# Hybrid encoder layer on one core: attention started behind V's projection, the convolution's taps set between its rows, 256 keys for every block of queries

## What is computed

```python
xn = rmsnorm(x, g_mix)
proj = xn @ w_in + b_in                       # 1024 -> 512 a, 512 g, 512 q, 512 k, 512 v
u = a * sigmoid(g)                            # conv half
u = depthwise_conv(u, conv_w, 31 taps) + conv_b
conv_out = silu(layernorm(u) * ln_g + ln_b)
# attention half: 8 heads of 64; a query at column c sees all 8 rows and the 16 columns
# around c (clipped at the edges); bias from rpb by row and column distance
s = q @ k * 64**-0.5 + bias ; p = softmax(s) ; na_out = p @ v
h = x + concat(conv_out, na_out) @ w_out + b_out
h = h + moe(rmsnorm(h, g_ffn))                # 32 experts, 4 per token, clamped SwiGLU, 1024 wide
out = rmsnorm(h, g_final)
```

## Time and profile before

| | before |
|---|---|
| median of 3 runs | 1552.27 us (1552.17 to 1552.35) |
| the profiled execution | 1550.96 us, span 1549.1 us |
| PE / DVE / ACT / POOL busy | 1419.8 / 1316.0 / 960.7 / 332.5 us |
| last product of the projection ends | about 138 us |
| first scores read by DVE | 189.75 us |
| last product of the out-projection | about 322 us |
| last token's experts chosen | about 346 us |
| first expert's first weights on PE | 375.7 us |

### The profile page before, as it was taken

How to read it: one execution, slowest core, us unless ns; L and a number is a source line. 1 busy time by engine, 2 the same in 40 slices (tenths; PEclk the granted TensorE clock), 3 DMA queues, 4 the chain that set the end, 5 groups by cost and what they waited for, 6 DMA issues and landing times.

```text
span 1549.1 us, 19123 instructions
## 1 busy us (share of the span) xinstructions
PE 1419.8 (92%) x6476; PEld 1163.5 (75%) x6476; DVE 1316.0 (85%) x975; ACT 960.7 (62%) x707; POOL 332.5 (21%) x248
## 2 busy tenths in 40 slices
PE   5995179975899999999999999999999999999995
PEld 4884047764788888888888888888888888888874
DVE  7799543347899999999999999999999989999997
ACT  3230062232677777777777777777777777777762
POOL 5296760011111111111111111111111111111062
PEclk9998559965999999999999999999999999999998
DMA  9801320055899999999999999999999999999983
GB/s 301 311 1 28 106 97 1 1 206 202 317 377 389 389 374 383 391 382 386 395 382 385 384 391 377 381 389 385 390 378 396 382 387 379 393 374 390 389 323 96
DMA packets 85042, 479.81 MB, mean 310 GB/s; under 512 B 10731, under 2 KB 11030, under 8 KB 35862
## 3 DMA queue, kind: packets, MB, share of 16 engines
q1 hardware_dynamic: 71902, 433.14, 72.1%
q0 software_dynamic: 6944, 25.18, 4.7%
q10 hardware_dynamic: 6168, 21.13, 3.5%
HBM read 450.08 MB, written 29.33 MB: 309 GB/s over the span
## 4 chain that ended last, share of the span: by engine, by line
PE 82%; POOL 6%; DVE 4%; issue 3%; DMA 2%; ACT 2%; SPq 1%; POOLq 0%; ACTq 0%; DVEq 0%
PE pair L1691 22%; PE pair L1689 22%; PE pair L1690 22%; POOL area_t L582 3%; PE pair L1509 2%; PE pair L1510 2%; PE pair L1511 2%; PE pair L1702 2%; PE pair L1676 2%; PE pair L1669 2%; PE pair L1551 1%; DVE w_low L1184 1%; POOL ring L582 1%; PE pair L1570 1%; SPq L462 1%
## 5 line engine op out<-in xcount | busy, mean ns | idle before, releaser
L1184 DVE TENSOR_TENSOR w_low<-w_raw,w_high 128x2048 fp32r<-128x2048 f32 x380 | 864.0, 2291 | 91.7 <-ACT w_high L833 87.7
L833 ACT CAST w_high<-w_raw 128x2048 fp32r<-128x2048 f32 x380 | 728.1, 1917 | 283.4 <-PE pair L1691 283.4
L1689 PE MATMUL pair<-w_high,xT_high 128*128 128x512 f32 x1040 | 409.4, 394 | 0.0
L1691 PE MATMUL pair<-w_high,xT_low 128*128 128x512 f32 x1040 | 406.8, 391 | 0.0
L1690 PE MATMUL pair<-w_low,xT_high 128*128 128x512 f32 x1040 | 405.9, 390 | 0.0
L1691 PEld LDWEIGHTS pair<-w_high,xT_low 128*128 128x128 f32 x1040 | 196.1, 189 | 41.6
L1690 PEld LDWEIGHTS pair<-w_low,xT_high 128*128 128x128 f32 x1040 | 196.4, 189 | 40.3
L1689 PEld LDWEIGHTS pair<-w_high,xT_high 128*128 128x128 f32 x1040 | 196.3, 189 | 39.9
L1689 PE MATMUL pair<-w_high,hT_high 128*128 128x512 f32 x496 | 196.3, 396 | 0.0
L1690 PE MATMUL pair<-w_low,hT_high 128*128 128x512 f32 x496 | 193.6, 390 | 0.0
L1691 PE MATMUL pair<-w_high,hT_low 128*128 128x512 f32 x496 | 193.6, 390 | 0.0
(11 more groups left out here) (292 smaller groups left out, 1471.8 us busy)
## 6 DMA issues: line engine op xcount, KB each, us to landing
w_raw<-in_w_gate SPq DMA_DIRECT2D x128, 1024.0 KB, 7.2
w_raw<-in_w_up SPq DMA_DIRECT2D x128, 1024.0 KB, 6.5
w_raw<-in_w_down SPq DMA_DIRECT2D x128, 1024.0 KB, 7.2
y_rows<-area_m ACTq DMA_DIRECT2D x30, 512.0 KB
ring<-in_w_in SPq DMA_DIRECT2D x5, 2048.0 KB, 19.0
y_rows<-area_t SPq DMA_DIRECT2D x1, 8704.0 KB
ring<-in_w_out SPq DMA_DIRECT2D x2, 2048.0 KB, 10.5
h<-in_x SPq DMA_DIRECT2D x4, 512.0 KB, 8.8
```

Source lines behind the costliest of these rows:

```text
L833: s.copy(w_high[:, i % HIGH_RING, :], w_raw[i][:, :]).then_inc(high_ready, 1)
L1184: v.tensor_tensor(w_low[i][:, :], w_raw[i][:, :], w_high[:, i % HIGH_RING, :].bitcast(F32), ALU.subtract).then_inc(low_ready, 1)
L1689: t.matmul(to[half], tok_high, hi, start=(opens and kk == 0), stop=False)
L1691: last = t.matmul(to[half], tok_low, hi, start=False, stop=(k == KD - 1))
```

## The change

- POOL keeps only the norms' small operations up to the experts. All low parts of w_in and w_out, the tables and the scaling of LayerNorm go to DVE; SiLU is one ACT function (no Sigmoid and no multiplications on POOL); b_out is no longer added to h but enters each out-projection as one more matmul (`bout_rows`, L1601), split by one ACT and one DVE instruction.
- Every block now has 256 keys. For a middle block these are its own 128, the half block to its right and the half block to its left (`spans`, `v_mix`). A table then has 192 + 64 entries for the middle blocks.
- The taps are written out singly (`taps`) and spread: 67 between the low parts and tables of the projection's groups, 21 behind them, and two behind each of the first 18 rows of scores.
- The attention's loop on PE starts behind V; V's last block comes behind the first two pairs of scores. Scores of two heads are issued together (`qk_pair`), into four banks. All copies of transposed rows are ACT's.
- LayerNorm's steps stand inside the attention's loop (mean at step 16, variance at 21, SiLU at 28, low part at 31).
- The whole out-projection comes behind the attention's loop: first the attention half of all four blocks (each in its own two banks), then the convolution half, with `turn_xn2` (transposes for the router) between.
- SP loads expert piece 0 ahead of the out-projection's end, and pieces 1 to 4 behind it (before: 0 to 2, then 3 and 4).

The core of the diff:

```diff
-            for g_i in range(8, 20):
-                loaded, high, low = split_parts(g_i)
-                pool.wait_ge(win_high_ready, g_i + 1)
-                g.tensor_tensor(low, loaded, high.bitcast(F32), ALU.subtract).then_inc(win_low_pool, 1)
...
+            def tables(hd):
...
+                dve.wait_ge(raw_loaded, 16 * N_ROWS * (hd // 2 + 1))
+                raw = raw_bias[:, hd % 2, :].rearrange("p (r w) -> p w r", r=N_ROWS)
+                for dst, first, o, w in ((T_mid[:, hd, 0:192], QB, 0, 192), (T_mid[:, hd, 192:256], QB // 2, 192, 64),
+                                         (T_edge[:, hd, 0, :], QB, 256, 256), (T_edge[:, hd, 1, :], 0, 512, 256)):
+                    v.tensor_tensor(dst.rearrange("p (w r) -> p w r", r=N_ROWS), raw[:, first:first + w // N_ROWS, :],
+                                    mask[:, o:o + w].rearrange("p (w r) -> p w r", r=N_ROWS),
+                                    ALU.add).then_inc(tables_ready, 1)
...
+            glu(3)
+            for g in range(9, 16):
+                win_low_part(g)
+                taps(2)
+                if g % 2:
+                    tables(g - 9)
+                    tables(g - 8)
+                taps(2)
+            for g in range(16, 20):
+                win_low_part(g)
+                taps(2)
+            taps(CONV_K * CC - 2 * TAP_STEPS - taps_made[0])
...
+            for i in range(NS + 6):          # DVE
+                n = normalised_at(i, 10)
+                if n is not None:
+                    normalise(n)
                 if i < NS:
                     scores(i)
+                if i < TAP_STEPS:
+                    taps(2)
...
+                if i == CENTRE_AT:
+                    dve.wait_ge(mean_done, 1)
...
+                if i in RECIP_AT:
+                    dve.wait_ge(std_ready, 1)
...
+            for n in range(NQ - 1):          # PE
+                project_v(n)
+            pe.wait_ge(act_evac, 12)
+            qk_pair(0)
+            qk_pair(2)
+            project_v(NQ - 1)
+            pe.wait_ge(act_evac, 16)
             for i in range(NS + 5):
+                if i < NS:
+                    transpose_p(i)
+                if i % 2 == 0 and i + 4 < NS:
+                    qk_pair(i + 4)
+                if 1 <= i <= NS:
+                    pv(i - 1)
+                n = normalised_at(i, 10)
+                if n is not None:
+                    transpose_o(n)
+                if i == MEAN_AT:
+                    pe.wait_ge(conv_tap, CONV_K * CC)
+                    pe.wait_ge(attn_low_ready, 4)
...
+                if i == VAR_AT:
+                    pe.wait_ge(squared, CC)
+                    pe.wait_ge(attn_low_ready, 8)
...
+                if i == NS + 1:
+                    pe.wait_ge(s_ready, NS)
+                    project_attn(0)
+                if i == NS + 2:
+                    project_attn(1)
+                    pe.wait_ge(pT_ready, NS)
+            project_attn(2)
+            project_attn(3)
...
+            project_conv(0)
+            project_conv(1)
+            turn_xn2(0)
+            project_conv(2)
+            turn_xn2(1)
+            project_conv(3)
```

More of the change, by code:

```diff
@@ L469, in _ @@
             sp.dma_start(unit(6), wout_v[:, :, 0:HALF]).then_inc(wout_loaded[0], 16)
-            for i in range(3):
-                load(i, 0)
+            sp.dma_start(bout_raw, bass.AP(b_out.tensor, b_out.offset, [[0, 64], [1, D_MODEL]])).then_inc(bout_loaded, 16)
+            load(0, 0)
             sp.wait_ge(wout_done, 2 * NQ)
-            for i in (3, 4):
+            for i in (1, 2, 3, 4):
                 load(i, 0)
@@ L570, in _ @@
[L570 to L594, removed]
@@ L743, in _, with exp_row, v_out, wout_high_part @@
                 s.activation(kT[:, i, :], bank[i][:, :], ACT.Identity, bias=colT[:, 12 + i:13 + i]).then_inc(act_evac, 1)
[L744 to L748 removed]
+            def exp_row(i):
+                act.wait_ge(neg_max_ready, i + 1)
+                if i >= 3:
+                    act.wait_ge(p_transposed, i - 2)
+                s.activation(P_sb[:, i % 3, :], S_sb[:, i % 3, :], ACT.Exp, bias=neg_max[:, i:i + 1],
+                             accum_out=row_sum[:, i:i + 1]).then_inc(exp_ready, 1)
+            def v_out(n):
+                act.wait_ge(proj_done, 16 + n + 1)
+                rows = slice(P // 2, P) if n < 2 else slice(0, P // 2)
+                s.copy(v_mix[rows, n % 2, :], bank[4 + n][rows, :])
+                s.copy(v_sb[:, n, :], bank[4 + n][:, :]).then_inc(act_evac, 1)
+            def wout_high_part(p):
+                half, c = WOUT_PARTS[p]
                 act.wait_ge(wout_loaded[half], 16)
@@ new lines, in tap, with taps @@
+                taps_made[0] += 1
+                next_tap[c], last_tap[c] = k + 1, taps_made[0]
+            def taps(count, known=CC):
+                for _ in range(count):
+                    left = [c for c in range(known) if next_tap[c] < CONV_K]
+                    tap(min(left[0:2], key=lambda c: last_tap[c]))
+            def tables(hd):
+                if hd == 0:
+                    dve.wait_ge(mask_step, 15)
+                    dve.wait_ge(y_stored, 16)
+                    dve.wait_ge(proj_done, 8)
+                dve.wait_ge(raw_loaded, 16 * N_ROWS * (hd // 2 + 1))
[5 more added lines that the diff above has]
+                                    ALU.add).then_inc(tables_ready, 1)
@@ L1054, in _ @@
             win_low_part(5)
+            taps(9, known=1)
             glu(1)
@@ L1170, in _ @@
             dve.wait_ge(router_loaded, 32)
-            residual(NQ - 1, 0)
+            residual(0, 0)
+            residual(0, 1)
             norm2(0)
-            residual(NQ - 1, 1)
+            residual(1, 0)
+            residual(1, 1)
             norm2(1)
+            xn2T_first(0)
+            residual(2, 0)
+            residual(2, 1)
+            xn2T_first(1)
+            norm2(2)
+            residual(3, 0)
+            residual(3, 1)
             top(0)
-            norm2(2)
             top(1)
+            xn2T_first(2)
             norm2(3)
             top(2)
+            xn2T_first(3)
             top(3)
@@ new lines, in project_conv @@
+            def project_conv(n):
+                pe.wait_ge(conv_low_ready, CC)
+                pe.wait_ge(wout_low_ready, 8)
+                tokens = slice(n * P, (n + 1) * P)
+                for half in range(2):
+                    to = bank[OUT_BANKS[n][half]][:, :]
+                    for k in range(CC):
+                        t.matmul(to, conv_high[:, k, tokens], wout_high[half][:, k, :], start=False, stop=False)
+                        t.matmul(to, conv_high[:, k, tokens], wout_low[half][:, k, :], start=False, stop=False)
+                        last = t.matmul(to, conv_low[k][:, tokens], wout_high[half][:, k, :], start=False, stop=(k == CC - 1))
+                    last.then_inc(wout_done, 1)
@@ L1602, in _ @@
+            for n in range(NQ - 1):
+                project_v(n)
[3 more added lines that the diff above has]
+            project_v(NQ - 1)
             pe.wait_ge(act_evac, 16)
```

425 lines of the change are left out of this document (197 added, 228 removed).

## The result

The changed kernel took 1497.88 us as the median of four runs (1493.63 to 1501.43), against 1552.22 us for the kernel before; the ratio is 0.9658, with a 95% interval of 0.9639 to 0.9677. The forecast was 1492, with a range of 1474 to 1512. The profiled execution took 1493.63 us (span 1491.7), 57.3 less than that of before. Its four times lie in two places: 1493.6 and 1494.4 at a mean granted clock of 0.964 and 0.962, and 1501.4 twice at 0.955.

What follows compares the result with a forecast made beforehand. PE bounds the experts, so time could come only from the 376 us ahead of them: last choice at 286 instead of 345.9, 60 us off 1550.96 gives 1491, with the median 1.3 above it 1492; range 1474 to 1512.

Steps and rivals of the forecast that it cites:

- A, first scores: DVE's queue of low parts, taps and tables ahead of attention: first scores at 140.3 us instead of 189.75.
- POOL off: POOL's removed work counts as nothing by itself; without POOL beside it a DVE tap takes 0.69 us.
- B, 16 steps of 1.97: Attention loop up to LayerNorm's mean: PE at half clock, DVE and ACT hidden, 1.97 us a step, ending at 177.5.
- C, last product with V: LayerNorm's chain inside the attention loop: last product with V at 229 (half clock) or 213 (full clock), taken as 223.
- D, 48 us for the out-projection: Out-projection on PE: 200 products of 0.232, 46.4 us, plus 1.6 for starting at half clock, ending at 271.
- E, 15 us: From out-projection's end to the last choice of experts: 15 us (12 to 24) instead of 23.8, at 286.
- To the first expert, nothing: From the last choice to the first expert's product nothing changes; the weight pieces' 22 us of loading are hidden.
- a drain behind each load: ACT's table switches in LayerNorm: a 1380 ns drain was left out; with it four switches add at most 5.5 us.
- The first rival: PE's clock stays up through the attention loop: last product with V at 213, 1481 us; chance 0.18.
- the second: The chain through the attention loop is longer: 1505 to 1530, taken as 1512; chance 0.16 together with the fourth.
- the third: Something other than POOL doubles DVE's taps, so all cost 1.40 and the kernel is slower: 1606 us; chance 0.04.
- the fourth: Two heads' scores run one after the other: 0.6 us more a step, 13 to 19 us; 1505, inside the second.

Runs made afterwards that it cites:

- Experiment 8: Changed kernel plus 12 POOL subtractions of 128x1024 whose result nobody uses, with ACT's copies of V waiting for them: 1518.86 us.
- experiment 4: Changed kernel with all 124 taps ahead of the first scores and none between the rows of scores (TAP_STEPS 18 to 0): 1523.06 us.
- experiment 6: Changed kernel with the second head's scores issued behind a product with V instead of beside the first head's: 1510.13 us.
- experiment 1: The changed kernel run again without any edit: 1494.94 us, ratio 0.9654 to the kernel before.
- experiment 9: Changed kernel with three weight pieces (7 to 9) issued only behind the gather of the first expert's tokens: 1496.3 us.

## Why the prediction was right, step by step

- **A, first scores, 140.3: 137.13.** Right, and for the reason given. The 3.2 us between them are several small terms: the work began at 71.6 and not 72.9 (1.3), the 57 taps took 37.4 us and not 39.3 (1.9), the 11 low parts 1.14 each and not 1.19 (0.6), the tables 0.4 less; two waits for the tables' loads, called just hidden, took 0.8 back. Two heads' tables took 79.46 - 76.13 = 3.33 us, 1.67 a head against 1.7, so the strided rate was the right row (below). That a stride past a 16-byte line is paid for is also what the Trainium skill ("SBUF — State Buffer", section "Door 1: The DMA port swizzle") says. The forecast's "5 us less" without it holds only if the 0.2 us for four instructions goes too; the rates alone give 8 x 768 x 0.6 ns = 3.7.

```profile
76.13 0.68 DVE L1035 TENSOR_TENSOR area_t<-area_m 128x192 f32<-128x192 f32 x2 [0.48 <-DMA area_m<-rpb_pad]
...
79.46 1.42 DVE L1014 SCALAR_TENSOR_TENSOR area_m<-area_u,convT,area_m 128x512 f32<-128x512 f32 x2
```

- **POOL off.** Priced at nothing for itself and 0.69 for each tap. Experiment 8 shows what it carries: twelve POOL instructions beside DVE put the first scores 18.6 us back. Of the 52.6 us of A, experiment 4 gives 24.8 to the 36 taps that now stand behind the first scores (161.96 without that move); the other 27.8 are POOL's absence and the scores' place ahead of mean and centring, and no run parts these.
- **B, 16 steps of 1.97: 143.09 to 174.53, 1.96 each.** The number was right by luck, and half of the reason. I had PE at half clock throughout and DVE hidden below it. PE's clock in that stretch was 0.81, and DVE, busy 29.34 of the 31.44 us, set the pace with its 1.85 and small waits. At half clock throughout the same way takes 35.3 us (experiment 4), not 31.5: 16 times the step left out a ninth pair of scores and a 17th row's transposes ahead of the mean, the transposes of the first block's result (0.9 us) and the wait for its division (0.5). That omission and the wrong clock, nearly 4 us each, cancel. The idle time of PE that I then took for room cost me experiment 6.

```profile
143.09 0.44 PE L1567 MATMUL pair<-ident,area_m 128*128 128x128 f32 x2 [1.59 <-ACT area_v L707]
...
174.53 4.51 PE L1641 MATMUL pair<-area_m,mean_w 128*128 128x512 f32 x8
```

- **C, last product with V, 223: 220.5.** The 223 was chosen between two sums, 229 at half clock and 213 at full clock. Mean and variance took 4.5 us each instead of 5.8, at a clock of 0.77 and 0.81 (174 to 179 and 188 to 193 us), in part at full clock; the square root ended at 196.6 (forecast 204), SiLU at 212.57 (219.5). From there it took 7.9 us, where the sum for half clock had 9.5.
- **D, 48 us for the out-projection: 52.6.** The term was too small by 4.6. I had counted 200 products and not the transposes that stand between them: 16 of xn2 (2.1 us) and four of the last attention block (0.6), and the half clock at its start, 1.9 us instead of 1.6. The rest stands around the eight products of b_out: the way from the product before it to the second behind it is 0.4 us longer than three plain steps of 0.227 (239.07, 239.39, 239.82, 240.15 are the starts of one case), 3.2 us in all, and the plain products, at 0.227 instead of 0.232, give back 1.1.
- **E, 15 us: 12.2.** Too large by 2.8, so that the last choice came at 285.25, against 286. In experiment 1 the same stretch took 16.3, so that the term is good to a few us either way.
- **To the first expert, nothing: +3.2**, the gather (PE waited 6.71 us for it, before 3.58). I had asked whether the four pieces arrive in time, not whom they disturb on the way. In experiment 1 the 29.8 came out as 29.7.
- The rule of the Trainium skill ("ScalarE: Activation LUTs", section "What ACT_TABLE_LOAD costs") with a drain behind each load was left out of the sum. All four loads of the loop took 1.28 us and the next instruction began within 0.02 us: no drain is visible here.

The profiled execution was 1493.63, 2.6 above the 1491 of the sum: -3.2 at A, +0.7 from there to the last product with V, +4.6 at D, -2.8 at E, +3.2 at the gather. That so little is left is in part luck, since the single errors have both signs. The rest up to 1497.88 is the spread of the times, which goes with the mean clock (0.955 in the long ones) and which the forecast had as a range and not as two places; the second median of 1494.94 lies nearer. The first rival (clock up throughout) was wrong as a whole and right for part of the loop; the second did not occur; the third was refuted by experiment 8, the fourth, made by hand in experiment 6, cost 15 us where the forecast had 13 to 19. In the third, 18 steps of 1.33 more are 24 us and not the 21 written there; its later sum did use 24.

## What to carry to other kernels

Before work is put between the steps of a loop, compare its engine's pace with the step of the slowest neighbour at the clock that this one will get: here DVE with two taps needs 1.85 us and PE at half clock 1.95, and 36 taps between 18 rows were free. Taken out they cost more than their own length: PE then rested for 24 us and ran the loop at half clock. That the rest alone brought the half clock is not shown, since experiment 6 fell to it without one. Idle time of PE at full clock need not be room for more PE work: price the step at half clock first. Of steps that no row needs yet (SiLU, reciprocals), put them behind the last row that would queue behind them: that was worth 7.7 us here, with one line.

## What the runs showed of the hardware

- POOL slows DVE by more than a share: a 128x512 tap goes from 0.69 to 2.32 us beside 128x1024 subtractions of POOL (2.46 us each), and to 1.40 beside the low parts of the kernel before. The other way, one table addition of 384 keys on POOL took 31.96 us beside taps, and others of its form, beside taps too, 1.66 to 5.33; no run explains the difference.
- The scores of two heads, each on 64 of the 128 rows of PE, take together what one takes: 1.33 us at half clock.
- PE, busy without a gap in the attention's steps, stayed at half clock for 40 us in experiment 6; in the changed kernel, where the same steps had gaps, it was granted 1.00 in some stretches of 4 us and 0.50 in others. No run explains when it changes.
- A gather took 8.6 and 9.8 us from issue to landing while weight pieces kept the DMA engines at a share of 0.97 and 1.01, and 4.1 to 4.4 in the other profiles read for it (experiment 9).
